# Conditioning in full fp32 on four strips of the array's columns, and two slots of their own for the turned probabilities of the differential attention

## The reference, cut to what matters

```python
silu_c, silu_cc = silu(c), silu(c_ctx)            # [1, 1024] and [1024]
for l in range(2):
    mod   = silu_c  @ w_ada[l] + b_ada[l]         # 6 * 1024 values: shift, scale, gate, twice
    mod_c = silu_cc @ w_ada[l] + b_ada[l]
    a = rms_norm(h, g_mix[l]) * (1 + scale1) + shift1
    # mixer: Fourier mix, differential attention, neighbourhood attention,
    # each gated and projected, then w_out
    h = h + gate1 * mixer(a)
    h = h + gate2 * conv_ffn(rms_norm(h, g_ffn[l]) * (1 + scale2) + shift2)

def diff_attend(q, k, v, lam):                    # 4 heads, two maps a head
    s = q @ k.T / 8
    p = softmax(s)
    return (p[map 0] - lam * p[map 1]) @ v
```

## Time and profile before

| what | us |
|---|---|
| median of 3 runs | 2817.81 |
| lowest, highest | 2815.05, 2819.06 |
| profiled execution, its time | 2816.66 |
| profiled execution, its span | 2814.9 |
| TensorE busy (matmuls) | 2607.1 |
| VectorE busy | 1692.4 |
| ScalarE busy | 1310.4 |
| POOL busy | 187.3 |
| mean granted TensorE clock | 0.968 of full speed |

### The profile page before, as it was taken

The page is one execution under the profiler, slowest core; times in us unless marked ns, Lnnn a source line. Parts: engine busy times, 40 slices in busy tenths (PEclk is TensorE's granted clock), DMA queues, the critical chain, the costliest instruction groups (busy, mean ns, idle before and its releaser), DMA issues.

```text
span 2814.9 us, 42255 instructions
## 1 busy us (share of the span) xinstructions
PE 2607.1 (93%) x17744; PEld 2295.4 (82%) x17744; DVE 1692.4 (60%) x2778; ACT 1310.4 (47%) x2123; POOL 187.3 (7%) x239
## 2 busy tenths in 40 slices
PE   5997899998999998899989989999799999989999
PEld 2875677776777776878889989999699999976999
DVE  5345535545776666464657877666566675766665
ACT  5235534433444343454546554445444453555543
POOL 0000000000000000100000011010010110025100
PEclk8998999999999999899999999999899999999999
DMA  7124332222343543323454545553255456530554
GB/s 238 60 71 146 124 114 88 70 91 68 126 159 120 164 138 117 98 83 108 126 165 158 187 150 189 187 172 122 75 195 186 154 188 195 171 118 16 168 192 135
DMA packets 337389, 382.14 MB, mean 136 GB/s; under 512 B 7408, under 2 KB 301296, under 8 KB 337200
## 3 DMA queue, kind: packets, MB, share of 16 engines
q1 hardware_dynamic: 334656, 370.37, 40.4%
q0 software_dynamic: 2544, 9.06, 1.0%
HBM read 378.36 MB, written 1.05 MB: 135 GB/s over the span
## 4 chain that ended last, share of the span: by engine, by line
PE 74%; DVE 12%; ACT 10%; issue 2%; DMA 1%; POOL 0%; DVEq 0%; ACTq 0%; POOLq 0%
PE PS L1188 20%; PE PS L1190 19%; PE PS L1189 19%; ACT WH L1544 4%; DVE WL L1868 3%; PE PS L1205 1%; PE PS L1206 1%; PE PS L1207 1%; DVE TMP L1935 1%; PE PS L1237 1%; PE PS L1304 1%; PE PS L1219 1%; PE PS L1220 1%; PE PS L1297 1%; PE PS L1279 1%
## 5 line engine op out<-in xcount | busy, mean ns | idle before, releaser
L1868 DVE TENSOR_TENSOR WL<-RAWB,WH 128x1024 fp32r<-128x1024 f32 (+1 forms) x709 | 848.4, 1206 | 604.1 <-ACT WH L1544 603.2
L1188 PE MATMUL PS<-AH,WH 128*128 128x256 f32 (+1 forms) x3072 | 973.3, 317 | 79.0 <-DVE AL L1940 31.0
L1190 PE MATMUL PS<-AH,WL 128*128 128x256 f32 (+1 forms) x3072 | 953.0, 310 | 0.0
L1189 PE MATMUL PS<-AL,WH 128*128 128x256 f32 (+1 forms) x3072 | 952.2, 310 | 0.0
L1544 ACT ACTIVATE WH<-RAWB 128x1024 fp32r<-128x1024 f32 (+1 forms) x709 | 722.5, 1035 | 268.6 <-PE PS L1190 227.9
L1188 PEld LDWEIGHTS PS<-AH,WH 128*128 128x128 f32 x3072 | 584.3, 190 | 149.1 <-issue 44.8
L1190 PEld LDWEIGHTS PS<-AH,WL 128*128 128x128 f32 x3072 | 584.6, 190 | 32.2
L1189 PEld LDWEIGHTS PS<-AL,WH 128*128 128x128 f32 x3072 | 585.2, 191 | 31.3 <-issue 0.8
L1188 PE MATMUL PS<-BH,WH 128*128 128x256 f32 (+1 forms) x1504 | 472.6, 314 | 8.1 <-DVE BL L2041 3.0
L1190 PE MATMUL PS<-BH,WL 128*128 128x256 f32 (+1 forms) x1504 | 460.3, 306 | 0.0
L1189 PE MATMUL PS<-BL,WH 128*128 128x256 f32 (+1 forms) x1504 | 459.4, 305 | 0.0
(11 more groups left out here) (309 smaller groups left out, 2511.6 us busy)
## 6 DMA issues: line engine op xcount, KB each, us to landing
RAWB<-in_f_in SPq DMA_DIRECT2D x88, 1024.0 KB, 5.1
RAWB<-in_w_in SPq DMA_DIRECT2D x52, 1024.0 KB, 5.1
RAWB<-in_w_ada SPq DMA_DIRECT2D x48, 1024.0 KB, 5.5
RAWB<-in_w_up SPq DMA_DIRECT2D x44, 1024.0 KB, 5.2
RAWB<-in_f_out SPq DMA_DIRECT2D x40, 1024.0 KB, 5.1
RAWB<-in_w_down SPq DMA_DIRECT2D x20, 1024.0 KB, 5.1
RAWB<-in_sb_qkv SPq DMA_DIRECT2D x12, 1024.0 KB, 5.1
RAWB<-in_w_out SPq DMA_DIRECT2D x8, 1024.0 KB, 5.0
```

What stands on the lines that cost most here:

```text
L1188: pe.matmul(out, h, xh[:, 0:T], start=k == 0, stop=False)
L1189: pe.matmul(out, h, xl[:, 0:T], start=False, stop=False)
L1190: i = pe.matmul(out, l, xh[:, 0:T], start=False, stop=k == g.kt - 1)
L1868: dve.tensor_tensor(c.part("WL", p), c.raw(p.slab)[:, k0:k1, c0:c1], c.part("WH", p).bitcast(F32), ALU.subtract).then_inc(up("lo", ("lo", ...
```

## The change

The conditioning's slabs have no cuts any more: they are not split, and TensorE reads them raw, in full fp32. `SC` holds plain fp32 values, two columns for each k, and 32 columns are the stationary operand, of which the first two count; block k goes to strip k mod 4 of the array's columns, so that the bank holds four partial sums on partitions 0, 32, 64 and 96 (and their neighbours), over four strips of 32 partitions. ScalarE copies all 128 partitions. In place of the transposes four matmuls with a selector (`ST[:, 28:30]`, ones at rows 0, 32, 64, 96 for c and one further for c_ctx) turn the rows and add the four strips at once. The turned probabilities of the differential attention get a ring of two slots in `BI`, the combination and the use come a tick later each, and the statistics have three sets. The biases of the neighbourhood attention are loaded when TensorE is past the differential attention.

```diff
@@ -316,11 +316,9 @@
             for half in range(2):
-                s = self.slab(("w_ada", l), 0, 8, (c + 2 * half) * 128, 256, [(0, 4, 0, 256), (4, 8, 0, 256)])
-                for i in range(2):
-                    p = self.piece(s, i)
-                    self.add("ada", (l, c), n=(half, i), b=b, p=p)
-                    self.done(p)
+                s = self.slab(("w_ada", l), 0, 8, (c + 2 * half) * 128, 256)
+                self.add("ada", (l, c), n=half, b=b, p=s)
+                self.used_raw.add(s.j)
                 self.tick()
@@ -338,11 +336,11 @@
 
-    def turned(self, id, w, nk):
+    def turned(self, id, w, nk, to):
         tb = self.banks.take()
...
         self.tmps.give(w, ("turn",) + id)
-        pt = self.sqs.take()
+        pt = to.take()
         self.add("pT", id, n=nk, b=tb, t=pt)
@@ -475,6 +473,7 @@
         obanks = {}
+        pts = Ring(self, 2, [("seq_dft", l, 3)], "BI")
         self.add("g_sub", (l,))
@@ -484,20 +483,20 @@
                 b, p = self.banks.take(), self.tmps.take()
-                self.add("da1", (l, h, qt, m), n=n, b=b, t=p, x=(h * nq + qt) % 2)
+                self.add("da1", (l, h, qt, m), n=n, b=b, t=p, x=(h * nq + qt) % 3)
                 self.banks.give(b, ("prob", l, h, qt, m))
                 out.append(p)
-            self.later(1, lambda: da2(u, n, out))
+            self.later(2, lambda: da2(u, n, out))
 
...
             p0, p1 = out
-            self.add("da2", (l, h, qt), n=n, t=(p0, p1), x=(h * nq + qt) % 2)
+            self.add("da2", (l, h, qt), n=n, t=(p0, p1), x=(h * nq + qt) % 3)
             self.tmps.give(p1, ("wts", "da", l, h, qt))
...
             def turn():
-                pt = self.turned(("da", l, h, qt), p0, n // 128)
-                self.later(1, lambda: values(u, n, pt))
+                pt = self.turned(("da", l, h, qt), p0, n // 128, pts)
+                self.later(2, lambda: values(u, n, pt))
             self.later(2, turn)
@@ -505,7 +504,7 @@
             self.add("da_pv", (l, h, qt), n=n // 128, b=obanks[h], t=pt)
-            self.sqs.give(pt, ("pv", "da", l, h, qt))
+            pts.give(pt, ("pv", "da", l, h, qt))
             if qt == nq - 1:
@@ -979,7 +978,7 @@
     def sq(self, s):
-        return self.m["SQ"][:, s.i, :]
+        return self.m["BI"][:, s.i * 512:s.i * 512 + 512] if s.home == "BI" else self.m["SQ"][:, s.i, :]
 
@@ -1113,7 +1112,7 @@
             if i == 0:
-                on.wait_ge(*at("fa", l, 3))
+                on.wait_ge(*at("mark", "pe", f"da{l}"))
             else:
@@ -1208,24 +1207,23 @@
         elif kind == "ada":
-            half, i = s.n
-            hi, lo = c.part("WH", s.p), c.part("WL", s.p)
-            out = c.bank(s.b)[0:4, half * 256:half * 256 + 256]
-            for f in s.b.was:
-                on.wait_ge(*at(*f))
-            on.wait_ge(*at("lo", s.p.p))
+            cols = slice(s.n * 256, s.n * 256 + 256)
+            for f in s.b.was:
+                on.wait_ge(*at(*f))
+            on.wait_ge(*at("raw", s.p.j))
             on.wait_ge(*at("cond"))
-            for k in range(4):
-                pe.matmul(out, sc_v[:, 4 * i + k, :], hi[:, k, :], start=i == 0 and k == 0, stop=False)
-                t = pe.matmul(out, sc_v[:, 4 * i + k, :], lo[:, k, :], start=False, stop=i == 1 and k == 3)
-            t.then_inc(up("acc", ("ada",) + id + (half, i), ("wdone", s.p.p)), 1)
+            for k in range(8):
+                strip = slice(k % 4 * 32, k % 4 * 32 + 32)
+                t = pe.matmul(c.bank(s.b)[strip, cols], SC[:, 2 * k:2 * k + 32], c.raw(s.p)[:, k, :], start=k < 4, stop=k > 3)
+            t.then_inc(up("acc", ("ada",) + id + (s.n,), ("used_raw", s.p.j)), 1)
         elif kind == "ada_turn":
...
             on.wait_ge(*at("ada_rows", *id))
+            on.wait_ge(*at("sel"))
             for j in range(4):
-                t = pe.transpose(c.bank(s.b)[:, 4 * j:4 * j + 4], c.sq(s.t)[0:4, j * 128:j * 128 + 128], ident[0:4, 0:4])
+                t = pe.matmul(c.bank(s.b)[:, 2 * j:2 * j + 2], c.sq(s.t)[:, j * 128:j * 128 + 128], c.m["ST"][:, 28:30], start=True, stop=True)
             t.then_inc(up("acc", ("ada_turn",) + id), 1)
@@ -1544,17 +1541,15 @@
             on.wait_ge(*at("side", "small"))
-            act.activation(sc_f[:, 0, :], c.sm("c"), ACT.Silu)
-            act.activation(sc_f[:, 1, :], c.sm("c_ctx"), ACT.Silu).then_inc(up("acted", ("silu_c",)), 1)
-            on.wait_ge(*at("silu_c"))
             on.wait_ge(*at("zero"))
-            act.activation(sc_v[:, :, 0], sc_f[:, 0, :], ACT.Copy)
-            act.activation(sc_v[:, :, 1], sc_f[:, 1, :], ACT.Copy).then_inc(up("acted", ("cond_hi",)), 1)
+            for i, name in enumerate(("c", "c_ctx")):
+                t = act.activation(m["SC"][:, i:16:2], c.sm(name), ACT.Silu)
+            t.then_inc(up("acted", ("cond",)), 1)
         elif kind == "ada_rows":
-            on.wait_ge(*at("ada", *id, 1, 1))
+            on.wait_ge(*at("ada", *id, 1))
             for f in s.t.was:
                 on.wait_ge(*at(*f))
-            act.activation(c.sq(s.t)[0:4, :], c.bank(s.b)[0:4, :], ACT.Copy).then_inc(up("acted", ("ada_rows",) + id), 1)
+            act.activation(c.sq(s.t), c.bank(s.b)[:, :], ACT.Copy).then_inc(up("acted", ("ada_rows",) + id), 1)
         elif kind == "sq":
@@ -1870,27 +1863,24 @@
             dve.memset(EPS[:, 1:2], 1e-5).then_inc(up("vec", ("eps",)), 1)
-            dve.memset(m["SC"][:, :].bitcast(F32), 0.0).then_inc(up("vec", ("zero",)), 1)
+            dve.memset(m["SC"][:, :], 0.0).then_inc(up("vec", ("zero",)), 1)
             on.wait_ge(*at("side", "small"))
...
             t.then_inc(up("vec", ("half_bias",)), 1)
-            on.wait_ge(*at("cond_hi"))
-            dve.tensor_tensor(sc_v[:, :, 2], sc_f[:, 0, :], sc_v[:, :, 0].bitcast(F32), ALU.subtract)
-            dve.tensor_tensor(sc_v[:, :, 3], sc_f[:, 1, :], sc_v[:, :, 1].bitcast(F32), ALU.subtract).then_inc(
-                up("vec", ("cond",)), 1)
+            on.wait_ge(*at("side", "consts"))
+            strips = c.cc("ident").rearrange("p (q r) -> p q r", q=4)[:, :, 0:2].rearrange("p q s -> p s q")
+            dve.tensor_reduce(ST[:, 28:30], strips, AX.X, ALU.add).then_inc(up("vec", ("sel",)), 1)
         elif kind == "ada_turn":
...
             bias = c.sm(f"b_ada{l}", n, 4)[:, :, None].to_broadcast([128, 4, 2])
-            o = c.bank(s.b)[:, 0:16].rearrange("p (n s) -> p n s", s=4)
+            o = c.bank(s.b)[:, 0:8].rearrange("p (n s) -> p n s", s=2)
             x = MOD[:, l, n:n + 4, :]
...
             on.wait_ge(*at("ada_turn", *id))
-            dve.tensor_tensor(x, o[:, :, 0:2], bias, ALU.add).then_inc(up("vec", ("ada_bias",) + id), 1)
-            on.wait_ge(*at("ada_bias", *id))
-            dve.tensor_tensor(x, x, o[:, :, 2:4], ALU.add).then_inc(up("vec", ("ada_add",) + id), 1)
+            dve.tensor_tensor(x, o, bias, ALU.add).then_inc(up("vec", ("ada_add",) + id), 1)
             for first, dst, g in ((8, m["G1"], "g_mix"), (32, m["G2"], "g_ffn")):
@@ -1978,22 +1968,22 @@
             on.wait_ge(*at("score", *id))
-            if u > 1:
-                on.wait_ge(*at("prob", l, (u - 2) // nq, (u - 2) % nq, 1))
+            if u > 2:
+                on.wait_ge(*at("prob", l, (u - 3) // nq, (u - 3) % nq, 1))
             dve.tensor_reduce(ST[:, col:col + 1], c.bank(s.b)[:, 0:s.n], AX.X, ALU.max, negate=True).then_inc(
...
             on.wait_ge(*at("prob", *id, 1))
-            dve.reciprocal(ST[:, 8 + col:12 + col], ST[:, col:col + 4]).then_inc(up("vec", ("da_rec",) + id), 1)
+            dve.reciprocal(ST[:, 12 + col:16 + col], ST[:, col:col + 4]).then_inc(up("vec", ("da_rec",) + id), 1)
             on.wait_ge(*at("da_rec", *id))
-            dve.tensor_tensor(ST[:, 8 + col:9 + col], ST[:, 11 + col:12 + col], LM[:, 4 + id[0]:5 + id[0]], ALU.mult).then_inc(
+            dve.tensor_tensor(ST[:, 12 + col:13 + col], ST[:, 15 + col:16 + col], LM[:, 4 + id[0]:5 + id[0]], ALU.mult).then_inc(
                 up("vec", ("da_lam",) + id), 1)
             on.wait_ge(*at("da_lam", *id))
-            dve.tensor_scalar(p0[:, 0:n], p0[:, 0:n], ST[:, 9 + col:10 + col], None, ALU.mult).then_inc(
+            dve.tensor_scalar(p0[:, 0:n], p0[:, 0:n], ST[:, 13 + col:14 + col], None, ALU.mult).then_inc(
                 up("vec", ("da_p0",) + id), 1)
             on.wait_ge(*at("da_p0", *id))
-            stt(p0[:, 0:n], p1[:, 0:n], ST[:, 8 + col:9 + col], p0[:, 0:n], ALU.mult, ALU.add).then_inc(
+            stt(p0[:, 0:n], p1[:, 0:n], ST[:, 12 + col:13 + col], p0[:, 0:n], ALU.mult, ALU.add).then_inc(
                 up("vec", ("wts", "da") + id), 1)
@@ -2331,9 +2321,9 @@
                    G1=sb("G1", [128, 2, 8, 2]), G2=sb("G2", [128, 2, 8, 2]), ST=sb("ST", [128, 32]),
-                   LM=sb("LM", [128, 20]), SC=sb("SC", [128, 32], F32R), EPS=sb("EPS", [128, 4]), RAWB=sb("RAWB", [128, NR, SLAB]),
+                   SC=sb("SC", [128, 56]), EPS=sb("EPS", [128, 4]), RAWB=sb("RAWB", [128, NR, SLAB]),
```

(21 more changed lines are left out.)

## The result

| kernel | median us (lowest to highest, runs) | ratio to the kernel before, 95% interval |
|---|---|---|
| before | 2816.05 (2805.44 to 2819.06, 6) | |
| after | 2798.93 (2794.86 to 2806.61, 6) | 0.9948 [0.9926, 0.9971] |

The change makes the kernel about 15 us faster, where 65 were forecast and 2718 was the low and 2790 the high end of the range; the measured 2799 is above it. The direction was right, the size was not: about a quarter of it came.

The account below looks back on a forecast made before the run. TensorE was taken to bound the kernel (busy 2607.1 of 2814.9 us). Layer 0's attention -40, FFN -20, start -2 and layer 1 -3 make -65: forecast 2752 us, own range about 2725 to 2775, widened to 2718 to 2790 for rivals.

Parts of the forecast that it names:

- The slab on four strips: Conditioning matmuls: a slab in full fp32 takes 1.05 us instead of 1.92, gaining 0.87 us on each of 40 slabs.
- the turn: Turning the conditioning's rows: four selector matmuls take 0.93 us instead of 0.40, +4 us in the attention, +6 in the FFN.
- the start with both its halves: Start: first norm's squares 5.3 us earlier, 3.4 given back to three later splits of `w_in`; net -2 us.
- the FFN: Layer 0's conv FFN: -15 us of TensorE's work and -5 of idle, -20 together.
- the splits by themselves bring nothing: Removing 96 copies on ScalarE and 96 subtractions on VectorE (99 and 116 us) gains nothing itself; the effect is in waits.
- The splits that go: Conditioning splits removed: raw slabs arrive in time, 24 of 32 us idle goes in layer 0's attention, 5 of 13 in FFN.
- the whole term of 24 us of idle: Layer 0's attention: 24 of TensorE's 32 us of idle would go (bounds 5 and 30).
- the 6 us of clock: Layer 0's attention: 6 of the 13 us lost to half clock would come back (bounds 0 and 12).
- a sign of being wrong: FFN: new waits of L1188 for VectorE's split, with SP queued on a conditioning slab, would show the forecast wrong.
- the last rival: No change worth measuring: stalls of main slabs pinned behind raw ones in the FFN; about 2800 to 2817, 5 in 100.
- The attention's order: Turned probabilities in BI, combined and used later: layer 1's attention gains 3 us (bounds -4 and 7).
- the waits stay: Layer 0's attention: TensorE waits for other things instead, clock still falls, -24, -6 and -5 lost; 2787, 12 in 100.

Follow-up runs that it names:

- conditioning only: The change without its new attention order: order, slots and delays of the differential attention as in the kernel before; 2794.92 us, 0.9913 of the kernel before.
- Splits later: The whole change, with a split of an ordinary slab entering the list one conditioning slab later; 2806.00 us, 0.9953 of the kernel before.
- the queue cured: The change without its new attention order, with the 16 conditioning slabs of layer 0's attention issued from POOL's queue; 2754.15 us, 0.9773 of the kernel before.
- both stages on POOL's queue: The change without its new attention order, with conditioning slabs of layer 0's attention and FFN issued from POOL's queue; 2755.64 us, 0.9785 of the kernel before.
- order only: The kernel before with only the new attention order added, conditioning still split in high and low part; 2827.10 us, 1.0030 of the kernel before.

## Why the prediction was wrong

**Right.** The slab on four strips (1.05 forecast, 1.00), the turn (0.9, 0.89), the start with both its halves (-5.3 +3.4 forecast, -5.6 +3.4 measured), the FFN (-20, -19.3; of it 12.0 us are TensorE's busy time and 7.2 idle, where 15 and 5 were forecast), and that the splits by themselves bring nothing. By the 3.07 that the Trainium skill gives for four row tiles (TensorE: Matmul & The Clock Gate, Measured speedup vs the span model) the estimate for a slab was 1.27 us; here four strips are 3.57/1.00 = 3.6 times as fast as one. The Trainium skill also has weight loads overlap matmuls in flight only where the row groups differ (same title, The mechanism). This case disagrees: the strips share all 128 rows, and the 16 passes of a slab, each with its weight load, take 1.00 us. One thing in the prediction's rows is misplaced without effect on the sum: the stretch called half clock in the earlier trace rows begins 1.9 us late, hence its 0.64; from 215.4 to 222.2 the granted clock is 0.50.

**The step that failed** stands under "The splits that go", as "Is it there in time? [...] Covered." and under the order as "SP's queue gets waits for TensorE instead of VectorE; priced above." Only the conditioning slab's own arrival was priced: 9 to 13 us of cover against 5.5, which is so (no conditioning matmul waits for its slab in that stage). What was left out is who else is tied to that wait. SP issues in order, so the ordinary slab behind a conditioning slab goes out only once TensorE has used the conditioning slab three before, though "each kind stays in its own slot"; and with the conditioning's pieces gone ScalarE's list has the split at the same point, with the softmax behind it. This took the whole term of 24 us of idle and the 6 us of clock in layer 0's attention: TensorE idles 33.5 us in that stage after the change and 32.3 before, and the clock is 0.92 against 0.93. The runs show it in two ways: conditioning only, without the new order, has ScalarE's stops as well; and the conditioning slabs on a queue of their own take the stops away and give 40 us. Splits later shows that the place of the split in ScalarE's list is half of the matter.

With the queue cured that stage is 250.6 - 209.3 = 41.3 us shorter, where 40 were forecast: 19.5 us of TensorE's busy time (10 of work and 6 of clock forecast) and 21.8 of idle (24 forecast). So the terms were right for a kernel with a free queue, and not only their sum. The total is 2754, where 2752 was forecast, but of another kernel, without the new order.

The prediction came near the mechanism twice, each time for the FFN: as a sign of being wrong ("with SP queued on a conditioning slab"), and as the last rival, "main slabs pinned behind raw ones in the FFN" (2800 to 2817, 5 in 100). It is the other way round: in the FFN SP stands 325 us at conditioning slabs in the changed kernel (398 us at split slabs before), ScalarE stands 93 us at slabs under way, and TensorE waits 1.1 us for a split; both stages on POOL's queue gains nothing there. In the attention, where the kinds have slots of their own, the same thing cost 40 us.

**The attention's order** was forecast at -3 in layer 1 (bounds -4 and +7 of gain); it costs 10 to 15 us there: order only against before +14.7, and after against conditioning only +10.0. What was to be a gain had the wrong sign: the waits that it was to cure grew from 7.2 us to 11.9, and those of the head norm's sum from 0.9 to 3.7. The reason given here, that a tick is not a fixed stretch of work, is read from the plan; moving the sum a tick later took 3.8 of the 13.7 us away. The last part of it is the clock, 0.94 to 0.96 and 0.91 in the two windows of every kernel with the new order in layer 1. How much of that is the order's own stays open, since kernels with the old order there have 0.94 in the second window too (conditioning only) or 0.95 in the first (both stages on POOL's queue), and their stage varies from 124.1 to 129.6 us.

**The rivals.** The measured 2799 lies next to the last rival (2800 to 2817), which had the mechanism and the wrong stage, and 12 us above "the waits stay" (2787, 12 in 100). The latter's reason, latency of ScalarE, was half of it: the latency was ScalarE standing at a transfer. That the total came out near these numbers is also the doing of layer 1's attention, which none of them had.

## What to carry to other kernels

When a wait changes hands, price the whole queue that stands behind it, and not only the thing waited for: who issues it in order, what is issued after it, and which other engine has a step in its own list that needs that. When steps leave an engine's list, look at what moves up in their place. For a buffer held until its last use, instead of until a copy, try an issuing queue of its own: here it gave 40 us in one stage and nothing in another. And a delay counted in steps of a plan is worth only the work that really lies between the steps: read it off the list.

## What the runs showed of the hardware that was not expected

Four strips of 32 columns, each with its own weights and all 128 rows, run full fp32 matmuls of 256 columns side by side: 16 passes take 1.00 us, against 3.57 on one strip, filling and emptying included. The granted clock followed the waits closely: 0.93 in layer 0's attention before, 0.91 with conditioning only, 0.99 with the waits gone, so that of the 40 us that the queue gave, 25.5 are idle time and 14.3 are the same work done at a higher clock.
